# One more token block by rows in the expert scores, a shorter pair search, and dense sums held in PSUM

## The reference, cut to what matters

```
q = x @ w_pq                                  # 8 heads, two halves of 128
s1, i1 = top_k(q1 . keys1, 16); s2, i2 = top_k(q2 . keys2, 16)
top_s, pos = top_k(s1[:, None] + s2[None, :], 16)     # of 256 pairs
idx = i1[pos // 16] * 128 + i2[pos % 16];  g = softmax(top_s)
a = gelu(x . u[idx]) * g                      # 128 experts for each token
y = sum(a * v[idx]);  out = layer_norm(ALPHA * x + y)
```

## Time and profile before

| | |
|---|---|
| median of three runs | 3082.76 us |
| the profiled execution | 3082.5 us, its span 3080.7 us |
| TensorE busy | 2980.4 us (97%) |
| VectorE busy | 2327.8 us (76%) |
| ScalarE, GpSimd busy | 1204.8 us (39%), 1053.0 us (34%) |
| DMA | 693.46 MB, mean 225 GB/s |
| score stage of the experts | its first and last L1104 start at 741.8 and 1998.2 us |
| sum stage | its first and last L1443 start at 2005.8 and 3068.7 us |

### The profile page before, as it was taken

The page is one execution under the profiler, slowest core; times in us unless marked ns, Lnnn a source line. Parts: engine busy times, 40 slices in busy tenths (PEclk is TensorE's granted clock), DMA queues, the critical chain, the costliest instruction groups (busy, mean ns, idle before and its releaser), DMA issues. The chain is left out here.

```text
span 3080.7 us, 42384 instructions
## 1 busy us (share of the span) xinstructions
PE 2980.4 (97%) x15866; PEld 2565.9 (83%) x15866; DVE 2327.8 (76%) x4289; ACT 1204.8 (39%) x2245; POOL 1053.0 (34%) x750
## 2 busy tenths in 40 slices
PE   7997998999999999999999999979999999999998
PEld 6887886888888899989898999868888888888887
DVE  4214775567988888888887556569998998999898
ACT  2112332222222566656566657533333333333331
POOL 3222221001455443443434454424433333333331
PEclk9997998999999999999999999989999999999999
DMA  4223222222677666666666888789988898888881
GB/s 169 84 89 123 104 97 83 72 79 69 236 247 255 228 225 234 223 246 241 240 231 250 288 299 301 290 297 317 321 299 302 283 313 292 295 307 296 298 306 74
DMA packets 291846, 693.46 MB, mean 225 GB/s; under 512 B 20304, under 2 KB 134352, under 8 KB 288464
## 3 DMA queue, kind: packets, MB, share of 16 engines
q1 hardware_dynamic: 189776, 315.61, 30.7%
q0 software_dynamic: 73728, 268.47, 24.4%
q10 hardware_dynamic: 28160, 106.96, 9.0%
HBM read 564.08 MB, written 126.88 MB: 224 GB/s over the span
## 5 line engine op out<-in xcount | busy, mean ns | idle before, releaser
L1443 PE MATMUL y_ps<-v_hi,a_hi 128*128 128x512 f32 x1536 | 600.1, 391 | 20.4 <-DVE y L1572 11.5
L1444 PE MATMUL y_ps<-v_lo,a_hi 128*128 128x512 f32 x1536 | 599.6, 390 | 0.0
L1445 PE MATMUL y_ps<-v_hi,a_lo 128*128 128x512 f32 x1536 | 599.4, 390 | 0.0
L799 POOL TENSOR_TENSOR u_lo<-u_raw,u_hi 128x1024 fp32r<-128x1024 f32 x128 | 314.6, 2458 | 725.0 <-ACT u_hi L795 724.0
L1104 PE MATMUL z_first<-hT_hi,u_hi 128*128 128x512 f32 x1024 | 409.9, 400 | 9.5 <-PEq L825 5.1
L1508 POOL DMA_INDIRECT v_rows<-in_v,room x192 | 259.7, 1353 | 463.1 <-DVE y L1555 439.2
L1106 PE MATMUL z_first<-hT_hi,u_lo 128*128 128x512 f32 x1024 | 401.3, 392 | 0.0
L1105 PE MATMUL z_first<-hT_lo,u_hi 128*128 128x512 f32 x1024 | 400.7, 391 | 0.0
L1443 PEld LDWEIGHTS y_ps<-v_hi,a_hi 128*128 128x128 f32 x1536 | 289.6, 189 | 81.6 <-issue 11.9
L1445 PEld LDWEIGHTS y_ps<-v_hi,a_lo 128*128 128x128 f32 x1536 | 289.6, 189 | 60.4
L1444 PEld LDWEIGHTS y_ps<-v_lo,a_hi 128*128 128x128 f32 x1536 | 289.6, 189 | 60.3
(11 more groups left out here) (195 smaller groups left out, 5829.4 us busy)
## 6 DMA issues: line engine op xcount, KB each, us to landing
u_raw<-in_uT SPq DMA_DIRECT2D x128, 512.0 KB
room<-in_v SPq DMA_DIRECT2D x128, 512.0 KB
z<-z_sb ACTq DMA_DIRECT2D x128, 384.0 KB
gates<-g_sb ACTq DMA_DIRECT2D x24, 2048.0 KB
room<-z SPq DMA_DIRECT2D x16, 1536.0 KB
z_in<-z SPq DMA_DIRECT2D x16, 1536.0 KB
g_in<-gates SPq DMA_DIRECT2D x16, 1536.0 KB
room<-gates SPq DMA_DIRECT2D x15, 1536.0 KB
```

The costliest lines, as they stand in the source:

```text
L799: self.nc.gpsimd.tensor_tensor(self.u_lo[e][:], self.u_raw[e][:], self.u_hi[e][:].bitcast(F32), ALU.subtract).then_inc(self.u_lo_in[e], 1)
L1443: nc.tensor.matmul(o, ah, v_hi[p][:, i, c], start=(i == 0), stop=False)
L1444: nc.tensor.matmul(o, ah, v_lo[p][:, i, c], start=False, stop=False)
L1445: last = nc.tensor.matmul(o, al, v_hi[p][:, i, c], start=False, stop=(i == GROUP - 1))
```

## The change

Block 2 leaves the dense first product (`UB` 3, so z has 640 columns and the wide matmul 384) and goes by rows of u: 384 rows instead of 256, with another number per turn and six buffers, four rows ahead, two of them borrowed from the buffers of v. Its second product stays dense: gelu(dot) x gate is laid out over the experts in place of its gates, as before for `UB > GB` (code that was there and unused). In the last turn all rows are taken in the first 24 slots, and the first v tiles are loaded after the last dot.

The pair search keeps only the 80 of 256 sums that can be among the best 16 (row, column areas `KEPT`), and `decode` works out row and column from a position. Names are made by pairs of groups. In a turn the 32 pieces are laid into 28 slots; the softmax follows in slot 28, its Exp on ScalarE in slot 27. Blocks 0 and 1 leave one more group of names to the start of `experts_in`.

In `experts_out` the first and the last dense block keep two PSUM banks each over all 32 rounds and are added once, at the end. The other four are cycled forth and back over two pairs of banks, so that the block at a turning point goes on in the same banks: three additions of two banks a round instead of six. A bank pair is wanted again after one other block. ALPHA x h is folded into a block's first addition; h is loaded in four parts, the cycled blocks first. The scaling by one instruction remains for the two row blocks. ScalarE and VectorE make a in the order of the round before (`made`).

```diff
-UB = 2
+UB = 3
...
+    KEPT = [(0, 2, 16), (2, 2, 8), (4, 4, 4), (8, 8, 2)]
...
-        link(nc.vector.tensor_tensor(self.cand[:], bc(self.top[:, 0], 2, TOPK), bc(self.top[:, 1], 1, TOPK), ALU.add))
-        self.top16(link, self.cand[:].rearrange("p a b -> p (a b)"), self.cand_left[:],
-                   self.best[:, b % 2, h], self.pos[:, b % 2, h])
+        at = 0
+        for first, n, wide in self.KEPT:
+            part = self.cand[:, at:at + n * wide].rearrange("p (a c) -> p a c", c=wide)
+            last = nc.vector.tensor_tensor(part, bc(self.top[:, 0, first:first + n], 2, wide),
+                                           bc(self.top[:, 1, 0:wide], 1, n), ALU.add)
+            at += n * wide
+        link(last)
+        self.top16(link, self.cand[:], self.cand_left[:], self.best[:, b % 2, h], self.pos[:, b % 2, h])
...
+    def decode(self, link, b, half):
+        nc = self.nc
+        pos = self.pos[:, b % 2, half * PH // 2:(half + 1) * PH // 2]
+        row, col = self.ab[:, 0], self.ab[:, 1]
+        link(nc.vector.tensor_scalar(self.step, pos, 4, None, ALU.logical_shift_right))
+        link(nc.vector.tensor_scalar(self.step, self.step, 1, None, ALU.max))
+        nc.vector.tensor_scalar(self.past, self.step, 16, -16, ALU.mult, ALU.add)
+        link(nc.vector.tensor_scalar(self.step, self.step, -1, 5, ALU.mult, ALU.add))
+        link(nc.vector.tensor_tensor(col, pos, self.past, ALU.subtract))
+        link(nc.vector.tensor_tensor(row, col, self.step, ALU.logical_shift_right))
+        link(nc.vector.tensor_tensor(self.past, row, self.step, ALU.logical_shift_left))
+        link(nc.vector.tensor_tensor(col, col, self.past, ALU.subtract))
...
-        pos = self.pos[:, b % 2, hs]
-        nc.vector.tensor_scalar(self.ab[:, 0], pos, 4, None, ALU.logical_shift_right)
-        link(nc.vector.tensor_scalar(self.ab[:, 1], pos, 15, None, ALU.bitwise_and))
-        link(nc.vector.tensor_tensor(self.pick[:], bc(self.ab[:].rearrange("p a h k -> p a (h k)"), 3, TOPK),
+        ab = self.ab[:, :, 2 * (two % 2):2 * (two % 2) + 2].rearrange("p a h k -> p a (h k)")
+        link(nc.vector.tensor_tensor(self.pick[:], bc(ab, 3, TOPK),
...
-                    if h % 2:
-                        tk.names(link, b, h // 2)
+                    if h % 4 == 3:
+                        tk.decode(link, b, h // 4)
+                        for two in range(2):
+                            tk.names(link, b, h // 4 * 2 + two)
...
-    RING, EARLY = 3, 2
+    RING, EARLY = 6, 4
+    TOPK_SLOTS = 28
+    DOTS = UB * PH * TOPK - XU
     SLOTS = 32
-    PER_TURN = [24, 34, 27, 27, 27, 27, 45, 45]
+    PER_TURN = [48, 48, 42, 42, 42, 42, 62, 58]
...
-        rows_in = ahead.rows + [sb(f"u_rows{i}", [P, D]) for i in range(RING - len(ahead.rows))]
-        h_own = sb("h_own", [P, D])
-        kept = sb("kept", [P, 3, PH * TOPK])
+        rows_in = ahead.rows + ahead.v_raw
+        rows_in = rows_in + [sb(f"u_rows{i}", [P, D]) for i in range(RING - len(rows_in))]
+        h_own = tiles.h_own
+        kept = sb("kept", [P, 3, PH * TOPK]) if UB > GB else None
...
-            first = 6 if s == 0 else 0
-            before, n = sum(PER_TURN[:s]), SLOTS - first
-            return range(before + PER_TURN[s] * max(k - first, 0) // n, before + PER_TURN[s] * max(k + 1 - first, 0) // n)
+            first, end = 6 if s == 0 else 0, 3 * SLOTS // 4 if s == TB - 1 else SLOTS
+            n = end - first
+            at = [sum(PER_TURN[:s]) + PER_TURN[s] * min(max(j - first, 0), n) // n for j in (k, k + 1)]
+            return range(at[0], at[1])
+        def pieces_at(k):
+            return range(SLOTS * k // TOPK_SLOTS, SLOTS * (k + 1) // TOPK_SLOTS) if k < TOPK_SLOTS else range(0)
...
-                    elif n == 2:
+                    elif n == 3:
+                        sp.wait_ge(row_used, DOTS)
                         for e in range(2):
...
-                        if s < TB - 2 and k == SLOTS - 2:
+                        if s < TB - 2 and k == TOPK_SLOTS - 1:
...
-                    elif n == 6:
+                    elif n == 6 and q % 2:
+                        tk.decode(link, b, q // 2)
+                        tk.names(link, b, q - 1)
+                    elif n == 7 and q % 2:
                         tk.names(link, b, q)
-                    elif n == 7 and q == Q - 1:
-                        v.wait_ge(exps, b + 1)
-                        tk.gates(link, b)
...
-                    tk.names(link, b, PH // 2 - 1)
+                    tk.decode(link, b, 1)
+                    for two in range(Q // 2, Q):
+                        tk.names(link, b, two)
...
-                            top_piece(s, k // 8, k % 8)
+                            for n in pieces_at(k):
+                                top_piece(s, n // 8, n % 8)
+                            if k == TOPK_SLOTS:
+                                v.wait_ge(exps, s + 3)
+                                tk.gates(link, s + 2)
+                                if s + 2 < UB:
+                                    keep_picked(s + 2)
+                                nc.vector.engine_nop().then_inc(found_in, 1)
...
+        HELD = (0, DB - 1)
+        CYCLED = list(range(1, DB - 1))
+        LAST = len(CYCLED) - 1
+        def order(r):
+            if r == 0:
+                return [HELD[0], *CYCLED[:2], HELD[1], *CYCLED[2:]]
+            return [HELD[0], *(CYCLED[::-1] if r % 2 else CYCLED), HELD[1]]
+        def run(r, s):
+            return LAST * r + (LAST - CYCLED.index(s) if r % 2 else CYCLED.index(s))
+        def banks(r, s):
+            first = 2 * HELD.index(s) if s in HELD else 4 + 2 * (run(r, s) % 2)
+            return y_ps[first:first + 2]
+        def opens(r, s):
+            return r == 0 or (s not in HELD and run(r, s) > LAST * r)
+        def closes(r, s):
+            return r == NG - 1 or (s not in HELD and run(r, s) < LAST * (r + 1))
+        def made(r):
+            return order(max(r - 1, 0))
...
+                load_h(slice(GB + 1, TB - 1), cycled_here)
                 load_z(1)
-                sp.dma_start(y[:], d["h"].rearrange("n p c -> p n c")).then_inc(h_here, 16)
+                load_h(slice(0, GB), rows_here)
                 load_v(1)
+                load_h(slice(GB, GB + 1), held_here)
+                load_h(slice(TB - 1, TB), held_here)
...
+                            if s not in HELD and opens(r, s):
+                                wait(pe, y_read, 2 * run(r, s) + a - 3)
...
-                        nc.tensor.matmul(o, ah, v_hi[p][:, i, c], start=(i == 0), stop=False)
+                        nc.tensor.matmul(o, ah, v_hi[p][:, i, c], start=(opens(r, s) and i == 0), stop=False)
                         nc.tensor.matmul(o, ah, v_lo[p][:, i, c], start=False, stop=False)
-                        last = nc.tensor.matmul(o, al, v_hi[p][:, i, c], start=False, stop=(i == GROUP - 1))
+                        last = nc.tensor.matmul(o, al, v_hi[p][:, i, c], start=False,
+                                                stop=(closes(r, s) and i == GROUP - 1))
...
+                    held = s in HELD
+                    first = held or r == 0 or (r == 1 and s == CYCLED[-1])
+                    if held:
+                        v.wait_ge(held_here, 32)
+                    elif first:
+                        v.wait_ge(cycled_here, 16)
                     for a in range(2):
-                        n = BANKS * r + 2 * s + a
                         c = slice(a * 512, (a + 1) * 512)
-                        v.wait_ge(y_done, n + 1)
-                        nc.vector.tensor_tensor(y[:, GB + s, c], y_ps[n % 8][:], y[:, GB + s, c], ALU.add).then_inc(
-                            y_read, 1)
+                        part, o = y[:, GB + s, c], banks(r, s)[a][:]
+                        v.wait_ge(y_done, BANKS * r + 2 * order(r).index(s) + a + 1)
+                        if first:
+                            ins = nc.vector.scalar_tensor_tensor(part, part, ALPHA, o, ALU.mult, ALU.add)
+                        else:
+                            ins = nc.vector.tensor_tensor(part, o, part, ALU.add)
+                        ins.then_inc(held_read if held else y_read, 1)
...
-                v.wait_ge(h_here, 16)
-                nc.vector.tensor_scalar(y[:], y[:], ALPHA, None, ALU.mult).then_inc(h_scaled, 1)
-                v.wait_ge(h_scaled, 1)
                 for r in range(1, NG):
-                    for s in range(DB):
+                    for n, s in enumerate(made(r)):
+                        if r == 1 and closes(0, s):
+                            add(0, s)
...
+                        if r > 1 and closes(r - 1, s):
+                            add(r - 1, s)
+                        if n < GROUP:
+                            split_v(r, n)
+                        if n:
+                            lo(r, made(r)[n - 1])
+                        if r == 1 and n == 1:
+                            v.wait_ge(rows_here, 16)
```

(41 more changed lines are left out.)

73 lines of the change are left out of this document (34 added, 39 removed).

## The result

The changed kernel takes 3109.7 us (median, 3108.47 to 3113.18) against 3083.05 us (3079.69 to 3084.41) of the kernel before: a ratio of 1.0091, 95% interval 1.0076 to 1.0106. Forecast were 3066.5 us and a range of 3030 to 3100. It is slower, and outside the range. The profiled execution took 3109.49 us, its span is 3107.3.

What follows compares the result with a forecast made beforehand. VectorE was taken to bound turns 0 to 5, the DMA engines turns 6 and 7. Terms of -9 and -7 us took the 3080.7 us span to 3064.7, or 3066.5 us as measured time; range 3030 to 3100.

Steps and rivals of the forecast that it cites:

- Step 1: TensorE's score matmuls: 384-column ones take 0.174 us each; a turn with gates falls from 163 to 142.2 us.
- Step 2: VectorE's load in the score stage: 291 us for turns 0 and 1, 155.3 in each of turns 2 to 5.
- Step 3: Score stage: TensorE runs at most two or three slots ahead of VectorE; turns 2 to 5 take 158 us each.
- Step 4: Score stage's turns 6 and 7: DMA engines at 371 GB/s set 146 and 170 us, together 316.
- A: Turns 6 and 7 stay TensorE's, 284 us instead of 316; whole kernel 3034 us; chance 0.15.
- C: Turns 6 and 7 wait for rows of u at 321 GB/s, 361 us, +45: 3111 us; chance 0.18.
- rival B: Turns 6 and 7: transfers settle at 357 GB/s, together 328 us, 12 more: 3078.5 us; chance 0.17.
- Step 5: Dense sums in PSUM, output stage: nothing gained or lost in the steady part, -7 us at the start (0 to -14).
- Step 6: TensorE's clock may fall with waits in turns 0 to 5; costed at nothing.
- rival D: TensorE's clock at 0.8 in turns 2 to 5, +80 us: 3146 us; chance 0.04.

Runs made afterwards that it cites:

- e12: e7 with 45 instead of 60 dots in each of the last two turns, the last 30 rows left out: 3033.25 us, ratio 0.9844.
- e1: The changed kernel with the search's doubled slot moved to pieces 4 and 5, so no slot has two names steps: 3072.24 us, ratio 0.9967.
- e7: The changed kernel with names steps apart, row blocks' h loaded behind round 1's v tiles and row additions from round 2: 3058.68 us, ratio 0.9936.
- e3: The kernel before with the changed output stage (experts_out) alone: 3086.71 us, ratio 1.0018.
- e6: The changed kernel with all of e7's edits of the output stage, names steps not moved apart: 3098.93 us, ratio 1.0051.
- e11: The changed kernel with row additions begun in round 2 of the output stage, the loads' order untouched: 3100.57 us, ratio 1.0060.
- e10: The changed kernel with two blocks by rows instead of three and the old numbers of rows per turn: 3132.85 us, ratio 1.0166.
- e13: e10 with the two names steps apart: 3098.60 us, ratio 1.0061.

## Why the prediction was wrong

From the forecast's span of 3064.7 us to the measured 3107.3 there are 42.6 us: 39.1 by the start of turn 6 (1707.1 against 1668), -6.5 in turns 6 and 7 (1707.1 to the last score matmul at 2021.6, 314.5 against 5 + 316), +10.0 behind them (1085.7 against 1075.7).

**Step 1, right.** The 384-column matmuls stand 0.17 us apart at 2.4 GHz, and TensorE's own turn is 142 us where nothing holds it (e12, 141.90).

**Step 2, 5 us a turn too low.** Counted as the forecast did, with every wait taken off, VectorE's own share of a turn is 166.2 less 23.6/4, 160.3 us, forecast 155.3. Hold-ups beside u_lo explain 1 us of this: 8.0 us of them stood already in the 143.7 of the kernel before, which the forecast carried over, and the kernel after has 9.0. The rest is work. A dot behind a dot in one slot costs 1.37 us, not 1.15 (1194.41 and 1195.78), and ten slots a turn now have two: 2.2. A decode takes 1.81 (1179.43 to 1181.24), not 1.5, twice a turn: 0.6. About 1 us remains unassigned. Turns 0 and 1 were VectorE's, as forecast: TensorE waited 60.9 us for u_lo there, forecast 59 to spare.

**Step 3, the one that failed.** "From transposes to transposes: 26 x 5.23 + 3.6 [...] then 17.4 on TensorE: 158" (the terms add up to 157.0). Measured: 1046.42 to 1711.31 in four turns, 166.2 each, 33 us in all. In turn 2 the path holds up to the last hot matrix that it counts, slot 27's: TensorE takes it at 1182.31, 135.9 us behind its transposes at 1046.42, forecast 139.6. From there the forecast leaves VectorE out and puts TensorE at 17.4 us; measured are 30.3, up to the transposes at 1212.61. Slot 27's own pieces stand on VectorE ahead of the hot matrix of slot 28, 13.98 us from one to the other. TensorE waits 8.64 us for that matrix and goes on at the lower clock. The prediction had the pieces for it: names "4.1, up to 6 when held up", a decode of 1.5 and 32 pieces in 28 slots; it did not write down which slot gets which. In e1 the same stretch takes 21.5 us (1183.24 to 1204.74).

The other lump, in slot 13, makes TensorE stand just as long, but in turns 2 to 5 VectorE waits for other engines 0.9 us at most between its first hot matrix and that of slot 28. There it sets the pace whatever the order of its pieces, and TensorE's stall is time that it had to spare. That e1's turns of 156.0 to 157.7 meet the forecast's 158 is therefore in part luck: the forecast's sum holds 8 us a turn of hold-ups, e1 has 2, and the rest of e1's VectorE work is 5 us more than the forecast's. Turn 2's transposes came 6 us after the 1040 of the forecast; e1 has this delay too (1047.1), so it isn't the double step's. More of the slots there have two dots, which is some of it; the rest stays open.

**Step 4, right.** 314.5 us for 321. Turn 6 took 148.1 us in the kernel after and 146.8 in e7, forecast 146, with 54.44 MB at 370 GB/s, forecast 54.2 at 371. Rivals A (284) and C (361) fall. The Trainium skill (DMA: Bandwidth & Descriptors, "Where 436 GB/s comes from") puts transfers between HBM and SBUF at about 358 GB/s per core, which was rival B's price; here, with one core at work, 370 GB/s held over 147 us, and the measurement decides.

**Step 5, wrong by sign.** Forecast -7 us; alone it is +5 (e3). The steady part cost nothing, as forecast: no matmul waits for an addition after round 1. But of the start the prediction priced only bytes ("7.6 MB instead of 8.9"). It counted neither SP's 15.48 us for one issue ahead of the v tiles (the 7.11 us wait behind it is 3.94 where the load is moved, e6), nor the row additions (the 9.38 us wait goes without them, e11), which were ahead of a block's a that the new order wants second.

**Step 6, rival D at a smaller size.** The clock was costed at nothing where waits are hidden. It fell to 0.93 to 0.94 in turns 2 to 5, not 0.8, and cost 5 us of TensorE's time a turn; on the path only what lies behind slot 28's hot matrix counts. The Trainium skill (TensorE: Matmul & The Clock Gate, "A second HAM failure mode: psum-queue depth-cycling") tells of pauses between groups of matmuls that make the clock swing. The trace agrees as to the swing, but which pauses do it is the point: two of 9.4 us per turn gave 0.93 to 0.94, two of 3.5 gave 0.97 to 0.98 (e10), 20 of at most 3.9 in four turns 0.98 to 0.99 (e1).

## What to carry to other kernels

Where one engine feeds another through two buffers, write down the feeder's work slot by slot, and follow the path through the last slot in which the other still waits for it: a rounding such as `32 * k // 28` can put the two dearest pieces there. Whether a lump elsewhere costs anything depends on who has time to spare: 9 us a turn where the feeder was idle 40 us (e10 and e13), little where it never waits. In a start-up, price the issuing queue and the instructions ahead on the engine as well as the bytes. Count an engine's load as the turn less its waits, not as its busy time: VectorE was busy 154 of 166 us and waited for 5.9. And when an experiment gains more than its theory allows, look for what else it changed; here moving one piece by one slot was worth 37 us, and some 25 of these are VectorE's own share, which fell with the hold-ups.

## What the runs showed of the hardware

TensorE ran at 1.2 GHz for some 6 us (1194.86 to 1200.58) behind a stall of 8.64 us, and stalls of 3.5 us (e10) also lowered the clock. A VectorE operation with two SBUF inputs waited up to 2.2 us for GpSimd's u_lo, whose median is 2.39 us; a TENSOR_SCALAR with one input was held up as long (L756 in the kernel before, 2403 ns instead of 172). The 16 DMA engines moved 370 GB/s at a share of 0.97 over 147 us, most of it (31.99 of 54.44 MB) in gathers of rows.
